# One core, two attention stages: grouped attention worked token tile by token tile, modulation steps placed anew

## The reference

```python
c_act = jax.nn.silu(c)
for i in range(DEPTH):
    mod = c_act @ ada_w[i] + ada_b[i]
    sh1, sc1, g1, sh2, sc2, g2 = jnp.split(mod[:, None, :], 6, axis=-1)
    h = x * (1 + sc1) + sh1
    if i % N_MIXERS == 0:
        y = neighbourhood_mixer(h, na_w_qkv[j], na_rpb[j], na_w_o[j])
    else:
        y = gqa_mixer(h, cos, sin, gqa_w_qkv[j], gqa_q_norm[j], gqa_k_norm[j], gqa_w_o[j])
    x = layer_norm(DEEPNORM_ALPHA * x + (1 + g1) * y, ln_g[i, 0], ln_b[i, 0])
    h = x * (1 + sc2) + sh2
    y = hierarchical_moe(h, ...)
    x = layer_norm(DEEPNORM_ALPHA * x + (1 + g2) * y, ln_g[i, 1], ln_b[i, 1])
```

## Time and profile before

| | |
|---|---|
| three runs | 1721.78, 1724.84, 1724.46 us (median 1724.46) |
| profiled execution | 1723.27 us |
| its span, first to last instruction | 1721.5 us |
| mean granted TensorE clock | 0.926 of full speed |
| PE, DVE, ACT, POOL busy | 87%, 32%, 12%, 7% of the span |
| DMA | 534.33 MB, mean 310 GB/s |

### The profile page before, as it was taken

One profiled execution on the slowest core, in us unless ns is written; L12 is line 12 of the kernel. 1 busy time (PEld: TensorE's weight loads), 2 busy tenths in 40 slices (PEclk: granted clock), 3 DMA queues, 4 the chain that ended last, 5 costly groups with the idle time before them and its releaser, 6 DMA issues.

```text
span 1721.5 us, 27806 instructions
## 1 busy us (share of the span) xinstructions
PE 1499.0 (87%) x12504; PEld 932.6 (54%) x12504; DVE 546.5 (32%) x1206; ACT 210.0 (12%) x575; POOL 111.9 (7%) x109
## 2 busy tenths in 40 slices
PE   6998998898568999989988986977999988988994
PEld 3455444557456775656455642565665545554651
DVE  2564556451345511110110112585411110111013
ACT  2131112201112200000000000232200000000000
POOL 3111111200000020000000000300100000000001
PEclk8999998999779899999998998888899998998997
DMA  9544764663364779999999999544499999999994
GB/s 352 196 137 170 262 217 147 221 214 140 118 217 166 318 299 408 427 425 427 427 426 427 425 426 371 184 147 191 176 375 405 427 427 426 426 428 427 426 416 172
DMA packets 96886, 534.33 MB, mean 310 GB/s; under 512 B 5088, under 2 KB 7296, under 8 KB 73200
## 3 DMA queue, kind: packets, MB, share of 16 engines
q1 hardware_dynamic: 92992, 519.40, 75.3%
q0 software_dynamic: 3760, 13.00, 2.0%
HBM read 531.32 MB, written 1.05 MB: 309 GB/s over the span
## 4 chain that ended last, share of the span: by engine, by line
PE 63%; DMA 21%; DVE 11%; issue 2%; ACT 2%; POOL 1%; SPq 1%; DVEq 0%; ACTq 0%
PE bk L419 29%; PE bk L861 19%; DMA AR<-in_moe_w_down 13%; PE bk L893 7%; DMA ring<-in_moe_w_down 6%; PE bk L903 3%; DVE AR L979 3%; PE bk L415 2%; DVE mpart L987 2%; DVE AR L987 2%; ACT AR L1805 2%; PE bk L609 1%; DMA ring<-in_w_in 1%; POOL st L2144 1%; SPq L2293 1%
## 5 line engine op out<-in xcount | busy, mean ns | idle before, releaser
L419 PE MATMUL bk<-ring,AR 128*128 128x512 f32 (+2 forms) x1024 | 390.2, 541 | 14.9 <-DMA ring<-in_w_in 7.8
L861 PE MATMUL bk<-ring,AR 128*32 128x128 f32 x5120 | 307.3, 409 | 0.0
L419 PEld LDWEIGHTS bk<-ring,AR 128*128 128x128 f32 x1024 | 200.4, 198 | 189.3 <-issue 169.3
L861 PEld LDWEIGHTS bk<-ring,AR 128*32 128x32 f32 x5120 | 195.9, 127 | 95.5 <-DVE AR L979 4.5
L861 PE MATMUL bk<-AR 128*32 128x128 f32 x3072 | 187.1, 410 | 0.0
L979 DVE TENSOR_TENSOR AR<-bk,AR 128x128 f32<-128x128 f32 (+2 forms) x76 | 24.8, 326 | 504.3 <-ACT AR L1805 465.7
L1805 ACT ACTIVATE AR<-bk 128x128 f32<-128x128 f32 (+4 forms) x171 | 67.3, 409 | 961.1 <-PE bk L861 764.3
L893 PE MATMUL bk<-AR 128*32 128x512 f32 x368 | 145.6, 716 | 31.4 <-DMA AR<-in_moe_w_down 30.7
L893 PE MATMUL bk<-ring,AR 128*32 128x512 f32 x656 | 153.7, 699 | 15.6 <-DMA ring<-in_moe_w_down 15.5
L861 PEld LDWEIGHTS bk<-AR 128*32 128x32 f32 x3072 | 124.3, 127 | 53.8 <-DVE AR L979 4.5
L419 PE MATMUL bk<-AR,X 128*128 128x128 f32 x512 | 124.5, 412 | 0.2
(11 more groups left out here) (149 smaller groups left out, 1011.7 us busy)
## 6 DMA issues: line engine op xcount, KB each, us to landing
ring<-in_moe_w_gate SPq DMA_DIRECT2D x40, 2048.0 KB, 24.2
ring<-in_moe_w_up SPq DMA_DIRECT2D x40, 2048.0 KB, 20.6
ring<-in_moe_w_down SPq DMA_DIRECT2D x36, 2048.0 KB, 28.5
ring<-in_ada_w SPq DMA_DIRECT2D x24, 2048.0 KB, 10.4
AR<-in_moe_w_up SPq DMA_DIRECT2D x24, 2048.0 KB, 29.3
AR<-in_moe_w_gate SPq DMA_DIRECT2D x24, 2048.0 KB, 21.2
AR<-in_moe_w_down SPq DMA_DIRECT2D x20, 2048.0 KB, 28.2
ring<-in_w_in SPq DMA_DIRECT2D x12, 2048.0 KB, 10.5
```

Of the source, the lines that this page charges most:

```text
L419: ins = eng.matmul(o, l, r, start=i == 0, stop=i == len(pairs) - 1)
L861: ins = eng.matmul(o[32 * f:32 * f + 32, 128 * m:128 * m + 128], XG[u][:, c, 32 * j:32 * j + 32], w[:, c, f::4], start=c == 0, stop=c == N ...
```

## The change

1. **Modulation in the first block.** In `NA_ROUNDS` every tN of the rounds stands first in its round, one round earlier than it stood, and before the projections of that round; in `NA_SIDE` the pieces follow. `NA_LOADS` has new due times; ada pieces 14 to 17 now all go through one slot. t18 and t19 go behind the attention, into the new `output(0)`, and x18, x19 behind the router's count.
2. **VectorE's order in a round**, in all four attentions (the hybrid layers too): reciprocal, then `settle()`, then `scaled(i-3)`; before it was `scaled`, (copy,) reciprocal, `settle`.
3. **The grouped block by token tiles.** Ahead of the rounds stand only k0, k1, q00, K0, K1, q10, r00 (kN: key and value projection of token tile N; qjt: queries of half j, tile t; K, r: transposes). The other queries, the gate rows, the transposes of outputs and the first tile's four output quarters go into the rounds, all through bank 7. VectorE's `variance` and `rotate` go per tile into its side work. Both `pT` copies are ScalarE's. The second tile's output quarters follow in `output(1)`, 256 columns at a time, with t22 and t23. `ada(8)` for piece 20 goes ahead of the first variance; the loads are ordered anew.
4. **The second gate.** The rows of g2 go through bank 7 one after the other; in the second block they move from the router into the first quad of the experts.

```diff
-NA_ROUNDS = (("k2", "k3", "q2", "q3"), ("v00", "v10", "k4", "k5", "p04", "t13"),
-             ("v01", "v11", "k6", "k7", "p06", "t14"), ("v02", "v12", "t15"), ("v03", "v13", "t16"),
...
+NA_ROUNDS = (("t13", "k2", "k3", "q2", "q3"), ("t14", "v00", "v10", "k4", "k5", "p04"),
+             ("t15", "v01", "v11", "k6", "k7", "p06"), ("t16", "v02", "v12"), ("t17", "v03", "v13"),
...
-GQA_ROUNDS = ((), (), (), (), ("t20",), (), ("t21",), (), ("l",), ("t22",))
-GQA_SIDE = ((), ("+",), ("+",), ("+",), ("+",), ("x20", "+"), ("+",), ("x21", "n", "m", "+"), ("l", "+"), ("x22",))
+GQA_ROUNDS = (("q01",), ("r10",), ("q11",), ("r01", "t20"), ("t21",), ("r11", "g0", "g1", "g2", "g3"),
+              ("a00", "a01", "a02", "a03"), ("l", "o00", "o01"), ("o02", "o03"), ())
+GQA_SIDE = (("v10",), ("w10",), ("v01", "+", "w01"), ("+",), ("v11", "+", "w11"), ("x20", "+"), ("x21", "n", "+"), ("m", "+"),
+            ("l", "o00", "o01"), ("o02", "o03", "s"))
+GQA_LOADS = ((2, 14), (0, 39), (1, 52), ("ada", 20, 8), ("ada", 21, 53), ("wo", 0, 115), ("wo", 1, 123), ("ada", 22, 70),
+             ("ada", 23, 85))
...
+            def output(i):
+                raw_cols(i, 0)
+                for f in ("a10", "a11", "a12", "a13", "o10", "o11"):
+                    common(i, f)
                 logits(i, 0)
+                for f in ("o12", "o13"):
+                    common(i, f)
                 raw_cols(i, 1)
+                total(4 * i + 18, 6)
+                logits(i, 1)
+                total(4 * i + 19, 5)
...
+                fill_bank[0] = [4, 5, 6, 7]
+                for f in ("k0", "k1", "q00", "K0", "K1", "q10", "r00"):
+                    unit(f)
                 fill_bank[0] = [7]
...
+            def second_gates(i):
+                pe.wait_ge(*drained("adaT", 12 * i + 11))
+                for j in range(2):
+                    gate_rows("g2", i, 1, j, 7)
...
+                    if i >= 2:
+                        j, u = i - 2, i % 2
+                        v.wait_ge(*exps(tag, j))
+                        if j > 1:
+                            v.wait_ge(*drained("o", tag, j - 2))
+                        v.tell(eng.reciprocal(sm[:, u, 12:16], sm[:, u, 8:12]), sem("recip"), nth(tag, j))
+                    settle()
                     if i >= 3:
                         scaled(i - 3)
-                    if i >= 2:
-                        j, g, u = i - 2, groups[i - 2], i % 2
-                        if g["mask"] is None:
...
-                    settle()
```

More of the change, by code:

```diff
@@ L875, in experts @@
                         end(ins, "gsT", i, q)
+                        if i and not q:
+                            second_gates(i)
                     hidden(3)
@@ new lines, in out_quarter @@
+            def out_quarter(i, t, q):
+                o, f = slice(256 * q, 256 * q + 256), f"o{t}{q}"
+                v.wait_ge(*drained(TAG[i], "g3"))
+                v.wait_ge(sem("fin"), 2 * i)
+                v.wait_ge(*filled(TAG[i], f))
+                v.chain()
+                free(tt(TMP[:, 0:256], bank(TAG[i], f)[:, 0:256], GB_[:, o], ALU.mult), TAG[i], f)
+                v.chain()
+                ins = stt(X[:, t, o], X[:, t, o], ALPHA, TMP[:, 0:256], ALU.mult, ALU.add)
+                if q == 3:
+                    v.tell(ins, sem("raw"), 2 * i + t + 1)
+                else:
+                    v.step(ins)
+                if q % 2:
+                    v.chain()
+                    v.step(stats(t, q // 2, X))
@@ L1565, in router, with more @@
+                def more(f):
+                    if f[0] == "v":
+                        variance("q" + f[1:])
+                    else:
+                        rotate("q" + f[1:])
+                ada(8)
+                for f in ROPED[0:3]:
+                    variance(f)
+                    rotate(f)
+                todo = list(GQA_SIDE)
+                attend("gqa", lambda: side(1, todo.pop(0), more))
+                output(1)
             def router(i):
@@ L1934, in attend @@
                         j, g, u = i - 2, groups[i - 2], i % 2
-                        for b in range(g["nk"] // 128 if g["mask"] is not None else 1):
+                        for b in range(g["nk"] // 128):
                             s.wait_ge(*filled("pT", tag, j, b))
@@ L2029, in neighbourhood @@
                 attend("na", settle)
-                for f in ("a10", "a11", "a12", "a13"):
-                    take(f)
-                raw_cols(0, 1)
-                normed(0, 1)
+                output(0)
             def grouped():
@@ L2067, in router, with settle @@
+                for f in ("k0", "k1", "q00", "K0", "K1", "q10", "r00"):
+                    take(f)
+                todo = list(GQA_ROUNDS)
+                def settle():
+                    for f in todo.pop(0):
+                        if f[0] in "ga":
+                            common(1, f)
+                        elif f[0] not in "tlo":
+                            take(f)
+                attend("gqa", settle)
+                output(1)
             def router(i):
-                for j in range(2):
-                    s.wait_ge(*filled("g2", i, j))
-                    free(act(G2[j], bank("g2", i, j)[:, :], ACT.Copy), "g2", i, j)
+                if not i:
+                    second_gates(i)
```

486 lines of the change are left out of this document (197 added, 289 removed).

## The result

The changed kernel takes 1684.7 us (median; 1684.5 to 1686.8) against 1723.3 us: a ratio of 0.978 (0.976 to 0.980), 38.6 us less. The forecast was 1671, 13.7 us too low; the measured time lies inside its range (1646 to 1697). The profiled execution took 1684.54 us, its span 1682.7.

The account below looks back on a forecast made before the run. The prediction took TensorE and VectorE waiting on each other in the neighbourhood rounds as the bound, experts being bound by weight loads. From 1723.27, -48.8 (first block), -0.6 (hybrid layers) and -2.8 (grouped block) gave 1671 us, range 1646 to 1697.

Parts of the forecast that it names:

- The neighbourhood rounds: First block, first scores to last output: earlier totals remove TensorE's waits and low-clock excess, -52.4 us.
- The replay: Neighbourhood rounds replayed with VectorE's own durations: pieces 14 to 17 done at about 402, 419, 433, 446; no total waits.
- late-load rival (b): First block: loads of pieces 14 to 17 come late every round, half the gain stays away; 1695 us, chance 0.10.
- VectorE's order: Side work ahead of scaling: outputs wait only in short rounds; two `diag` waits go in the hybrid layers, -0.6 us.
- Up to the first grouped scores: Grouped block ahead of its rounds: only four products stand there, so the first scores come 17.0 us sooner.
- behind the last output: Grouped block, last output to first expert product: half the output projection and gate rows leave, -19.2 us.
- The grouped rounds: Grouped block's rounds: 65.7 us of work plus 21.6 of waits, 87.1 with overlaps taken off, +28.9 us.
- The clock: Grouped block: TensorE's clock drops at two waits in the new rounds, +4.5 us, bounds 0 and +12.
- Rival (d): Grouped block: the clock swings among short groups, half of (c)'s price, +33 less 4.5; 1700 us, chance 0.05.
- (c): Grouped rounds to gather: TensorE's clock drops at the first gap and stays low, +72 less 4.5; 1739 us, chance 0.04.
- a clock well under 0.8: Sign in the grouped rounds of the profile after that would speak for (c) or Rival (d).
- The second experts: Experts last as long as their weights (DMA share 0.99 in the first block's), so only their start counts: 0 us.

Follow-up runs that it names:

- experiment 4: Kernel before, with only totals t13 to t17 first and one round earlier, and VectorE's side work ahead of scaling in all four attentions: 1727.5 us, ratio 1.001.
- experiment 5: Kernel before, with t13 to t17 moved, VectorE's new order except in the grouped attention, and the changed kernel's `NA_LOADS`: 1695.8 us, ratio 0.983.
- experiment 1: Changed kernel with GpSimd's update of X moved back ahead of its six square roots: 1679.8 us, ratio 0.974.
- experiment 2: Changed kernel with GpSimd's four operations on X ahead of the second block's outputs cut to 16 of 1024 columns: 1679.4 us.
- experiment 6: On top of experiment 1, total t21 one round later, behind the gate rows: 1673.0 us, ratio 0.971.
- experiment 7: Changed kernel with the second block's second gate rows back in the router, t22 and t23 ahead of the last transposes: 1685.4 us, ratio 0.977.
- experiment 8: Changed kernel with the edits of experiment 1, experiment 6 and experiment 7 together: 1671.0 us, ratio 0.969.
- experiment 11: Changed kernel with the edits of experiment 8, plus VectorE's scaling ahead of side work in grouped rounds 3 to 6: 1673.2 us, ratio 0.970.

## Why the prediction was right, and where it was not

**The neighbourhood rounds: the size right, the reason too simple.** -52.4 was forecast, -53.2 came, and no total waits long. But the text let the totals' place take away all 45.3 us and gave the loads no share ("two of them would cost up to about 7 us"). Experiments 4 and 5 show that the place, with VectorE's order that goes with it, is worth 12.4 alone, and that the loads and the rest carry the other 41. The replay had used the new tables as a whole, and its times held: pieces 14 to 17 were done at 400.5, 417.9, 432.9 and 449.5, forecast 402, 419, 433 and 446. So the size was no luck; the account of the cause was short of the loads. The late-load rival (b) did not come true: VectorE's 9.09 us at one load was covered but for 1.6 us.

**VectorE's order: priced too kindly.** The step said that TensorE's output waits "only if a round is shorter" than VectorE's side work, and left the grouped rounds out. That is where rounds are short: experiment 4 shows +21 us there, in its slowest execution, with nothing else changed in that block. In the changed kernel, whose grouped rounds are longer, no output waits for a scaling. What the order did in the hybrid layers does not show: -1.9 us stands in the table, but the same stretch took 388.5 to 391.8 us with the new order and 390.6 before, and 390.6 in experiments 4 and 5. In the changed kernel the order can't be taken back as a whole: with the totals in front and `scaled` ahead of the side work, an extraction would wait for an output that stands behind the group which waits for that extraction.

**Up to the first grouped scores, and behind the last output: right.** -17.9 and -19.6 against -17.0 and -19.2. (The terms given for the first add to 1112.9, not 1113.4, half a microsecond.)

**The grouped rounds: the failed term.** Forecast +28.9 and +4.5 for the clock; +47.6 came. TensorE's waits sum to 26.1 us instead of 21.6, and its work takes 79.7 us instead of 65.7 at the full clock. Of the single waits most were right or too long (2.94 for the first exponentials, forecast 3.0; 3.5 for gate rows and transposes a, forecast 5.3). One was wrong: t21 with 12.67 us, which makes t20, t21 and r11 together 15.8 instead of 8.4. Its cause, for the 8.3 us of it that experiment 1 takes away, is the one instruction stream that the forecast did not price: the change moves GpSimd's update of X behind its six square roots, and so into the rounds. The list of the change does not name that move. The trace of before had the clue, in VectorE's eight products of 128x64 beside that same work:

```profile
1080.80 7.15 DVE L979 TENSOR_TENSOR AR<-cst,qkn 128x64 f32<-128x64 f32 x8
```
```profile
1077.94 9.38 POOL L2140 TENSOR_TENSOR X<-X,AR 128x1024 f32<-128x1024 f32 x4 [2.17 <-PE bk L415]
```
Experiments 1 and 2 set the collision's share at 5 to 8 us.

The Trainium skill, page "GPSIMD Engine Reference", section "1. Specifications", says that GpSimd's SBUF interface is shared with VectorE and that VectorE operations with two SBUF inputs contend with it. The runs agree: the slowed groups shown all read two tiles of SBUF, and they slow only beside GpSimd's work (6.39 against 2.23 us). The forecast could have found the place with it.

**The clock: a term that was too small by about 8 us,** and the largest part of the miss. Of the 14.0 us of excess work, about 12.2 are what the slow groups took above the same groups at the upper level (an estimate, summed over the profile's rows); the other 1.8 is work that was priced too low. The forecast had 4.5, bounds 0 and 12. The text tied the clock to long gaps. Experiment 1 takes most of the gap away and the low stretch stays as long; experiment 6 takes all but 2.32 us away and the clock still falls among groups that wait for one bank in turn. The trace of before shows a fall without a long gap too, ahead of the 5.50 us that the forecast read:

```profile
1169.26 2.65 PE L419 MATMUL bk<-AR 128*128 128x64 f32 x16 [1.65 <-ACT AR L1805]
1171.70 1.92 PE L415 MATMUL bk<-cst,AR 128*128 128x128 f32 x8
```
These transposes took 1.04 at the upper level, so the clock was down before the gap. Rival (d), the clock that swings among short groups, had this mechanism, but its price was too high: 33 us for rounds and outputs against about 12, and the half in it was the forecast's own guess (half of the 72 in (c) would be 36). By the forecast's own sign, a clock well under 0.8, neither (c) nor (d) came: the mean over the rounds is 0.82, and 0.80 over those of before. That the one bank does it, and not merely the sum of small waits, no run here shows.

**The second experts: the step that said "only their start counts" failed.** It read the DMA share of 0.99 as cover for the gate rows. Over the whole stage it is; in the first quad TensorE is what the loads wait for. Experiment 7 brings the loads back to 48.3 us after the start and 2.4 of the 4.0 us with it; in experiments 8 and 11, with the same move, the stage takes 476.3 and 475.5. Where the other 1.6 us come from stays open.

## What to carry to other kernels

- When work is moved in a queue that looks idle, look at what its instructions touch while they run: beside GpSimd's elementwise work VectorE's groups with two operands in SBUF took 1.9 to 6 times as long.
- A stage bound by DMA has a head in which the slots are still to be released; what is put there can shift what follows (2.4 of 4.0 us here), and no share over the stage shows that.
- An order that frees one chain (side work ahead of the scaling) needs rounds long enough to hide it. The order that goes with the first attention's new totals cost up to 21 us in the other attention when it came alone (experiment 4).

## What the runs showed of the hardware

- VectorE's six products of a rotation took 2.23 us alone and 6.39 beside GpSimd's work on other tiles; eight products of 128x64 took 1.16 and 7.15. GpSimd's four operations took 9.4 to 10.3 us beside it.
- The granted clock was 0.61 to 0.72 over 28 to 39 us, while TensorE was 79% to 84% busy with groups separated by waits of mostly half a microsecond, behind gaps of 2.32 to 12.67 us; in the kernel before it was 1.00 over a stretch that was 75% busy. Such a share, which the low clock itself raises, doesn't tell which of the two will come.
